# Expert routing on one core: gathers through DRAM exchanged for one-hot matmuls on tokens kept in SBUF

## The reference, cut to what is computed

```python
logits = (t @ w_router + b_router).astype(F32)
top_v, top_i = lax.top_k(logits, TOP_K)                      # 4 of 32
wts = jax.nn.softmax(top_v, axis=-1)
combine = jnp.sum(jax.nn.one_hot(top_i, N_EXPERTS) * wts[..., None], axis=1)
...
y = clamped_swiglu(t @ wu + bu) @ wd + bd                    # per expert: 1024 -> 2048 -> 1024
return acc + cw[:, None].astype(t.dtype) * y
...
x = x + gt2 * moe_ffn(h, ...)                                # then a final RMSNorm
```

## Time and profile before

| | us |
|---|---|
| median of three runs | 1377.89 |
| the profiled execution, its own time | 1376.65 |
| its span, first to last instruction | 1375.0 |
| first expert matmul starts | 366.82 |
| last down matmuls start, 16 records | 1330.96 |
| TensorE busy in the span | 1108.3 (81%) |
| VectorE, ScalarE, GpSimd busy | 274.8, 187.0, 124.5 |
| mean granted TensorE clock | 0.915 of full speed |
| bytes moved by DMA | 481.22 MB, mean 350 GB/s |

### The profile page before, as it was taken

One profiled execution on the slowest core, in us unless ns is written; L12 is line 12 of the kernel. 1 busy time (PEld: TensorE's weight loads), 2 busy tenths in 40 slices (PEclk: granted clock), 3 DMA queues, 4 the chain that ended last, 5 costly groups with the idle time before them and its releaser, 6 DMA issues.

```text
span 1375.0 us, 14665 instructions
## 1 busy us (share of the span) xinstructions
PE 1108.3 (81%) x5751; PEld 471.5 (34%) x5751; DVE 274.8 (20%) x597; ACT 187.0 (14%) x312; POOL 124.5 (9%) x195
## 2 busy tenths in 40 slices
PE   3699688884399888988888888888888888888872
PEld 0388565463133322322222322222222222322221
DVE  1310456465311100101110110101110110101116
ACT  2100632111001101010110101010110101010101
POOL 5000120013200001010000001010000101010003
PEclk8599879886699999999999999999999999999996
DMA  9844259226499999999999999999999999999964
GB/s 350 278 129 145 73 187 351 106 85 211 159 428 414 426 428 427 428 426 426 428 428 427 427 428 425 430 426 426 429 428 427 427 428 426 428 427 427 428 245 157
DMA packets 60656, 481.22 MB, mean 350 GB/s; under 512 B 9469, under 2 KB 21325, under 8 KB 32694
## 3 DMA queue, kind: packets, MB, share of 16 engines
q1 hardware_dynamic: 43936, 444.64, 78.0%
q0 software_dynamic: 10496, 24.18, 5.0%
q10 hardware_dynamic: 6198, 12.03, 2.4%
HBM read 467.38 MB, written 14.28 MB: 350 GB/s over the span
## 4 chain that ended last, share of the span: by engine, by line
DMA 60%; PE 28%; DVE 5%; issue 2%; ACT 2%; POOL 1%; ACTq 0%; SPq 0%; POOLq 0%; PEldq 0%; DVEq 0%
DMA arena<-in_w_up 29%; DMA arena<-in_w_down 28%; PE bank L1127 8%; PE bank L818 6%; PE bank L1147 5%; DMA ring<-in_w_ada 2%; PE bank L969 2%; PE bank L769 2%; PE bank L907 1%; PE bank L786 1%; PE bank L826 1%; PE bank L870 1%; POOL ring L539 1%; PE bank L1000 1%; DMA arena<-mods 0%
## 5 line engine op out<-in xcount | busy, mean ns | idle before, releaser
L1127 PE MATMUL bank<-ring,arena 128*64 128x512 f32 x1536 | 379.5, 641 | 91.0 <-ACT arena L745 51.2
L1127 PEld LDWEIGHTS bank<-ring,arena 128*64 128x64 f32 x1536 | 113.4, 147 | 329.8 <-issue 260.9
L1622 DVE TENSOR_SCALAR arena<-bank 128x256 f32<-128x256 f32 x64 | 24.2, 420 | 614.1 <-PE bank L1127 614.1
L769 PE MATMUL bank<-const,arena 128*128 128x128 f32 (+3 forms) x415 | 74.4, 319 | 77.1 <-DMA arena<-h_rows,idx 21.3
L1147 PE MATMUL bank<-arena 128*64 128x512 f32 x512 | 115.9, 595 | 20.9 <-DMA arena<-in_w_down 20.9
L1127 PE MATMUL bank<-arena 128*64 128x512 f32 x512 | 116.3, 597 | 16.5 <-DMA arena<-in_w_up 15.7
L1147 PE MATMUL bank<-ring,arena 128*64 128x512 f32 x512 | 116.1, 595 | 0.0
L769 PEld LDWEIGHTS bank<-const,arena 128*128 128x128 f32 (+3 forms) x415 | 58.5, 201 | 124.0 <-issue 69.9
L748 ACT ACTIVATE arena<-arena 128x512 f32<-128x512 f32 x32 | 20.2, 631 | 469.8 <-DVE arena L1622 469.8
L514 POOL DMA_DIRECT2D arena<-in_b_up x32 | 16.1, 503 | 745.9 <-PE bank L1147 745.9
L818 PE MATMUL bank<-ring,arena 128*128 128x256 f32 x352 | 81.1, 390 | 0.6 <-issue 0.6
(11 more groups left out here) (293 smaller groups left out, 726.6 us busy)
## 6 DMA issues: line engine op xcount, KB each, us to landing
ring<-in_w_up SPq DMA_DIRECT2D x96, 2048.0 KB, 25.2
arena<-in_w_up SPq DMA_DIRECT2D x32, 2048.0 KB, 28.1
ring<-in_w_down SPq DMA_DIRECT2D x32, 2048.0 KB, 24.3
arena<-in_w_down SPq DMA_DIRECT2D x32, 2048.0 KB, 25.4
ring<-in_w_ada SPq DMA_DIRECT2D x24, 1024.0 KB, 7.4
ring<-in_w_in SPq DMA_DIRECT2D x11, 1024.0 KB, 10.8
y_rows<-arena ACTq DMA_DIRECT2D x64, 128.0 KB, 8.3
ring<-in_w_out SPq DMA_DIRECT2D x4, 1024.0 KB, 5.7
```

The costliest lines, as they stand in the source:

```text
L769: return pe.transpose(out, in_, ident[0:rows, 0:rows])
L1127: mm = pe.matmul(B[2 * e + c % 2][64 * a:64 * a + 64, :], lhsT=xT[:, k, 64 * e:64 * e + 64], rhs=big(n)[:, CH * r + 512 * c:CH * r + 512 * ...
L1622: ins = dve.tensor_scalar(glu[:, 256 * b:256 * (b + 1)], u[:, :, 0], LIMIT, None, ALU.min)
```

## The change

Nothing of routing, token rows or expert outputs goes through DRAM any more.

- **Slots.** `rk1` holds rank + 1 of each token in each chosen expert, 0 elsewhere. For a pair, `build_rows` compares it with the constants 1..64 and gives G, a one-hot matrix tokens x 128 slots. After each pair the two columns are lowered by 64, for the next pass.
- **Picking.** h2 stays in SBUF. Instead of the gather and 8 transposes, `pick_up_rows` makes xT directly: for each of 8 k, three accumulating matmuls (prompt tiles of 128 tokens and the sample tile of 8) of h against G, into banks 0 and 1. It is done for the next pair in the middle of this pair's first down projection.
- **Returning.** GW = G times the routing weights is turned by three transposes (`turn_weights`) into Wc, slots x 264 tokens, copied by ACT. y is copied out to `ysb` by ACT and DVE, half each. `combine_step` multiplies Wc by ysb for the pair before, in four full matmuls of 512 columns and two with 32-column stationary tiles, spread over k = 2..6 of the first expert's up projection. DVE adds each of the five parts to `moe` or `moe_s`.
- **Biases.** b_up of a pair comes in one DMA; the bias of the down projection goes in once as a 33rd "expert": ysb starts as b_down, Wc as the routing weights by expert.
- **The end.** The last pair's sum, the residual and the gate are added on TensorE: six identity matmuls, then four and two of the last Wc. The first norm sums are taken in halves, and the stores are halved and shared by SP and ACT.
- **Layout.** Tiles of the loop lie elsewhere in the arena, which grows from 29300 to 29400 columns; POOL clears moe, moe_s and ysb, in place of the bias clears by DVE.

```diff
@@ picking (TensorE) @@
-                pe.wait_ge(sem("x_full"), it * 16 + 16)
-                pe.wait_ge(sem("gT_copied"), it * 2 + 1)
-                for k in range(KT):
-                    mm = turn(B[6 + k // 4][:, P * (k % 4):P * (k % 4 + 1)],
-                              xg.rearrange("p (c n r) -> p c r n", c=UPS, r=UP_ROWS)[:, c, r, :], P)
+            def pick_up_rows(pair_built):
+                pe.wait_ge(sem("g_built"), pair_built)
+                for k in range(KT):
+                    c, r = divmod(k, UP_ROWS)
+                    for t in range(3):
+                        mm = pe.matmul(B[k // 4][:, P * (k % 4):P * (k % 4 + 1)],
+                                       lhsT=h[0:NT[t], t, :].rearrange("p (c n r) -> p c r n", c=UPS, r=UP_ROWS)[:, c, r, :],
+                                       rhs=G[0:NT[t], t, :, :].rearrange("p e s -> p (e s)"), start=(t == 0), stop=(t == 2),
+                                       skip_group_check=True)
@@ returning (TensorE) @@
+                def combine_step(n):
+                    if n == 0:
+                        pe.wait_ge(sem("wc_copied"), it + 1)
+                        pe.wait_ge(sem("y_copied_a"), it * 2 + 1)
+                        pe.wait_ge(sem("y_copied_d"), it * 2 + 1)
+                    if n >= 2:
+                        pe.wait_ge(sem("sum_added"), it * 5 + n)
+                    if n < 4:
+                        t, a = divmod(n, 2)
+                        mm = combine(B[4 + n % 2][:, :], slice(P * t, P * (t + 1)), a)
+                    else:
+                        for a in range(2):
+                            mm = combine(B[4][32 * a:32 * a + 32, :], slice(S, S + 32), a)
+                    mm.then_inc(sem("sum_made"), 1)
...
+                        if e == 0 and 2 <= k < 7:
+                            combine_step(k - 2)
+                        if e and k == 2:
+                            turn_weights()
                         if e and k == 4:
                             turn_g(0)
...
-                    pe.wait_ge(sem(f"y_copied{e}"), it + 1)
-                    for a in range(2):
-                        pe.matmul(B[4 + e][64 * a:64 * a + 64, :], lhsT=one,
-                                  rhs=bias[e][:, FF2 + 512 * a:FF2 + 512 * (a + 1)],
+                    if e == 0:
+                        pe.wait_ge(sem("wc_copied"), it + 2)
...
                         if e == 0 and k == 4:
+                            pe.wait_ge(sem("u_read"), it * 2 + 2)
+                            pick_up_rows(it + 2)
                             turn_g(1)
@@ the loop's new work on DVE @@
+                dve.wait_ge(sem("xT_made"), it * 2 + 2)
+                dve.tensor_tensor(GW, G, wide(wd[:, :, pair].unsqueeze(3), 3, SLOTS), ALU.mult).then_inc(sem("gw_built"), 1)
+                dve.tensor_scalar(rk1[:, :, pair], rk1[:, :, pair], -float(SLOTS), None, ALU.add).then_inc(sem("rank_lowered"), 1)
+                build_rows(after).then_inc(sem("g_built"), 1)
+                for n in range(5):
+                    dve.wait_ge(sem("sum_made"), it * 5 + n + 1)
...
+                    dve.tensor_tensor(acc, acc, part, ALU.add).then_inc(sem("sum_added"), 1)
@@ POOL @@
-                    pool.dma_start(idx[:, :], list_dram[bass.ds(it * P, P), :]).then_inc(sem("idx_full"), 16)
-                    pool.indirect_dma_start(
-                        out=xg, out_offset=None, in_=h2_dram,
-            for t in range(3):
-                for k in range(TOPK):
-                    pool.indirect_dma_start(
-                        out=yk[t][k][0:NT[t], :], out_offset=None, in_=y_dram,
+                pool.wait_ge(chunks_used, it * PER + (PRE + 2 * UPS))
+                up_bias((it + 1) % PAIRS)
+            for t in range(2):
+                pool.tensor_tensor(moe[:, t, :], moe[:, t, :], gate2, ALU.mult).then_inc(sem("x2_part"), 1)
@@ ACT @@
-                for a in range(2):
-                    act.dma_start(y_dram[bass.ds(i * P + 64 * e, SLOTS), 512 * a:512 * (a + 1)],
+                    act.activation(ysb[r, e, :], B[4 + e][r, :], ACT.Copy).then_inc(sem("y_copied_a"), 1)
```

More of the change, by code:

```diff
@@ L236, in hybrid_layer @@
         wr = take(KT * E, z_at + 5 * D).rearrange("p (k e) -> p k e", k=KT)
[L238 to L259, removed]
+        bias = take(FF2, z_at)
+        ysb = take(2 * 512, z_at + 2 * D).rearrange("p (a n) -> p a n", a=2)
+        ysg = take(2 * 512, z_at + 3 * D).rearrange("p (a n) -> p a n", a=2)
@@ new lines, in hybrid_layer @@
+        xT = take(D, zs_at + 512).rearrange("p (k t) -> p k t", k=KT)
+        glu, lin, sg = (take(512, zs_at + 512 + D + 512 * n) for n in range(3))
+        gg = [take(512, hT_at + 512 * n) for n in range(2)]
+        gT = [take(512, hT_at + 1024 + 512 * n) for n in range(2)]
+        moe = take(2 * D, hT_at + 2304).rearrange("p (t c) -> p t c", t=2)
+        more_ring = take(4 * CH, ada_at)
+        gate2 = take(D, ada_at + 4 * CH)
+        rows2s = take(2 * D, ada_at + 4 * CH + D)
+        g_fin = take(D, ada_at + 4 * CH + 3 * D)
@@ L493, in _ @@
+            up_bias(0)
             pool.wait_ge(sem("npass_ready"), 1)
             passes = pool.value_load(npass[0:1, 0:1], min_val=1, max_val=MAXPASS)
[L495 to L502, removed]
-                    pool.dma_start(idx[:, :], list_dram[bass.ds(it * P, P), :]).then_inc(sem("idx_full"), 16)
-                    pool.wait_ge(sem("idx_full"), it * 16 + 16)
-                    pool.nop(nofuse=True)
-                    pool.indirect_dma_start(
-                        out=xg, out_offset=None, in_=h2_dram,
[L508 to L532, removed]
@@ new lines, in _ @@
+            with pool.Fori(0, total) as it:
+                pool.wait_ge(chunks_used, it * PER + (PRE + 2 * UPS))
+                up_bias((it + 1) % PAIRS)
+            pool.wait_ge(sem("sum_added"), total * 5 + 1)
+            for t in range(2):
+                pool.tensor_tensor(moe[:, t, :], moe[:, t, :], gate2, ALU.mult).then_inc(sem("x2_part"), 1)
+            for t in range(2):
+                pool.wait_ge(sem("x2_part"), t + 1)
+                pool.tensor_tensor(moe[:, t, :], moe[:, t, :], x[:, t, :], ALU.add).then_inc(sem("x2_part"), 1)
@@ L544, in _ @@
+            pool.wait_ge(sem("bias_full"), total * 16 + 16)
         @block.scalar
@@ L755, in _, with copy_rows @@
-            for n, t in enumerate(LAST):
-                act.wait_ge(sem("x2_ready"), n + 1)
-                act.activation(moe[0:NT[t], t, :], x[0:NT[t], t, :], ACT.Square,
-                               accum_out=ssum3[0:NT[t], t:t + 1]).then_inc(sem("sums"), 1)
-                act.wait_ge(sem("means"), 6 + n + 1)
-                root(t)
+            total = act.snap(passes * PAIRS)
+            def copy_rows(made):
+                act.wait_ge(sem("xT_made"), made)
+                act.activation(xT[:, 4:8, :], B[1][:, :].rearrange("p (k t) -> p k t", k=4), ACT.Copy).then_inc(sem("xT_copied_a"), 1)
@@ new lines, in _ @@
+            act.activation(sg[0:1, 0:1], root3[0:1, 0:1], ACT.Sqrt)
+            for t in range(2):
+                for a in range(2):
+                    act.wait_ge(sem("x2_made"), 2 * t + a + 1)
+                    act.activation(moe[:, t, 512 * a:512 * (a + 1)], B[2 * t + a][:, :], ACT.Square, accum_out=half_sum[:, t, a:a + 1]).then_inc(sem("half_sums"), 1)
+                act.wait_ge(sem("half_means"), t + 1)
+                act.wait_ge(sem("half_sums"), 2 * t + 2)
+                act.activation(root3[:, t:t + 1], half_sum[:, t, 1:2], ACT.Sqrt, scale=1.0 / D, bias=half_mean[:, t:t + 1]).then_inc(sem("roots"), 1)
@@ L763, in _ @@
+            act.wait_ge(sem("x2_ready"), 1)
+            act.activation(h[0:NB, 1, :], h[0:NB, 2, :], ACT.Square, accum_out=ssum3[0:NB, 2:3]).then_inc(sem("sums"), 1)
+            act.wait_ge(sem("means"), 7)
+            root(2)
+            for n in range(2):
+                act.wait_ge(sem("result"), n + 3)
+                act.dma_start(O["yp"][0, P:S, 512 * n:512 * (n + 1)], x[:, 1, 512 * n:512 * (n + 1)]).then_inc(sem("result_stored"), 16)
         @block.tensor
@@ L1556, in number @@
[L1556 to L1560 removed]
+                dve.wait_ge(sem("chosen_ready"), nth)
@@ new lines, in number, with weigh_tokens @@
+                link(dve.scalar_tensor_tensor(out=rk1[r, ts, :], in0=ranks.rearrange("p (t e) -> p t e", t=nt), scalar=1.0,
+                                              in1=chosen[r, ts, :], op0=ALU.add, op1=ALU.mult))
+            def weigh_tokens(ts, r, exps):
+                nt = len(range(3)[ts])
+                dve.wait_ge(sem("top_exp"), exps)
+                link(dve.tensor_tensor(wd[r, ts, :], ex[r, ts, :], chosen[r, ts, :], ALU.mult))
+                link(dve.tensor_reduce(tsum[r, ts], wd[r, ts, :], AX.X, ALU.add))
+                link(dve.reciprocal(tsum[r, ts], tsum[r, ts]))
+                link(dve.tensor_tensor(wd[r, ts, :], wd[r, ts, :], wide(tsum[r, ts].unsqueeze(2), 2, E), ALU.mult))
@@ L1596, in _ @@
```

(26 more changed lines are left out.)

341 lines of the change are left out of this document (146 added, 195 removed).

## The result

| | before | after |
|---|---|---|
| median, us | 1377.22 (4 runs) | 1386.26 (4 runs, 1384.93 to 1386.51) |
| span of the profiled execution | 1375.0 | 1384.5 |
| first expert matmul starts | 366.82 | 365.06 |
| from there to the last down matmul's end | 967.8 | 999.1 |
| from there to the end of the span | 40.4 | 20.4 |

The ratio is 1.0064, with a 95% interval of 1.0047 to 1.0082: slower by 0.6%, where 4.5% faster was forecast. The table already says where: the end gives back 20 us, where 18 were forecast, the start gives 1.8 instead of 9, and the loop, which was to give 34, takes 31.

What follows compares the result with a forecast made beforehand. The old loop was taken as DMA-bound, with TensorE some 15% below; after the change TensorE would narrowly decide. Start 357.5, loop 934, end 22 and 1.65 outside the span gave 1315 us, range 1292 to 1350.

Steps and rivals of the forecast that it cites:

- DMA per pair, 58.9 us: Loop: weights take the share freed by gathers, indexes and y stores, so a pair's transfers fall from 61.80 to 58.9 us.
- TensorE decides: Loop: with six chunks ready at the start, TensorE should hardly starve and sets the time, 16 x 58.4 = 934 us.
- TensorE per pair, 58.4 us: Loop: 46.2 us of remaining old work plus picking, combines, transposes and switches sum to 58.4 us a pair.
- Picking: Loop: 24 picking matmuls a pair at 0.272 us each, priced from L907, 6.5 us.
- Full combines and switches: Loop, per pair: four full matmuls 3.6 us, two with 32-column tiles 0.9, seven more switches between matmul kinds 0.7.
- The bounds: Loop: picking takes no less than 3.7 us a pair, and 12.4 if loads and matmuls run one after the other.
- rival 4: Loop: picks' loads don't hide, 12.4 instead of 6.5 us; 64.3 us a pair, 1410 us in all; chance 0.08.
- The start, 357.5: Before the loop: first up matmul at 357.5 us against 366.8, with the first picking slowed to 8.0 us.
- No waits, no clock loss in steady pairs: Loop: the 3.38 us wait for xT and its slow start go; new waits are covered, clock 1.00 in steady windows.
- rival 3: Loop: a new wait replaces the removed one; 1 to 3.4 us a pair gives 1331 to 1369 us; chance 0.15.
- The end, 22 us: After the last down matmul: 22 us to the end of the span, against 40.4; bounds 18 and 27.
- seven times: At the end: POOL's four operations of 1024 columns, 1.3 us each on DVE, may be seven times dearer.

Runs made afterwards that it cites:

- e3_no_returning: Changed kernel without the five combine steps and DVE's adds for all pairs but the last (result incomplete): 1320.09 us, one run.
- e6_all: Changed kernel with 128-row sample tile, three combine groups, 128-row up bias, POOL's last bias load left out: 1307.95 us, ratio 0.9504 to the kernel before.
- e2_pad: Changed kernel with the sample tile picked over 128 rows, the unfilled ones cleared, order unchanged: 1331.12 us, ratio 0.9676 to the kernel before.
- e5_group: Changed kernel with its five combine steps in three groups (two, two, one), same matmuls: 1375.44 us, one run.
- e1_order: Changed kernel with the same picks sorted by height, 16 of 128 rows, then 8 of 8 rows: 1359.27 us, ratio 0.9875 to the kernel before.

## Why the prediction was wrong, step by step

The profiled run took 71 us more than the 1315 forecast: 65 in the loop, 7.6 at the start, and 1.6 less at the end. Of the 65, 62 are 16 pairs at 62.27 instead of 58.4, and 3 are the slow first up matmuls.

- **DMA per pair, 58.9 us**: right. e3_no_returning and e6_all show 58.85 and 58.87.
- **"TensorE decides"**: right, and more than meant: no wait in the chain, DMA at 403 GB/s.
- **TensorE per pair, 58.4 us**: wrong, 62.27. This is the step that failed, by terms that were mis-sized. *Picking*, 6.5: measured 8.75. L907 is a run of equal 128-row matmuls, and for such a run its price was even 0.65 too high (5.85 in e2_pad). But every third pick has 8 rows, and the changes of height, which the sum put at nothing, cost 2.90. In all that is +2.25. *Full combines and switches*, 3.6 + 0.9 + 0.7 = 5.2: measured 4 x 1.06 + 0.98 + 5 x 0.15 (the up matmuls behind each visit) + 0.15 (those behind the three transposes) = 6.1, +0.9. " show none to speak of" looked at switches between tiles of one width; for a change of width the sum had only the transposes' 0.1 on entry, and I should have kept a higher bound. *The up bias*, not in the sum: I took off the down bias and did not see that the up bias went from 128 rows to one. The earlier trace rows have its old price, 1.72; the new is 1.86 and 1.87 behind it: +0.6. Together 3.75 of the 3.87 missing.
- **The bounds**: the 8.75 of picking lay between the bounds 3.7 and 12.4, and rival 4 named the point from which it decides, 62.2 us a pair; the pair took 62.27 and the kernel is 0.6% slower. That the point was met so closely is chance: it was the mark for loads that do not hide, and the missing time came from other terms. In e2_pad 48 loads of full tiles and their 48 matmul records fit in 5.85 us together. The Trainium skill, TensorE: Matmul & The Clock Gate, Part 3, "What overlaps and what doesn't", has loads overlap matmuls only in other row groups. By that the padded picks, all over the same 128 rows, could not overlap and would be dear; they are the cheap ones, so the trace disagrees. The outcome between my forecast and that rival had no case of its own, so the range ended at 1350.
- **The start, 357.5**: wrong, 365.06. TensorE began picking at 349.16, 0.5 late; then 15.04 us instead of 8.0, and 6.24 for 16 records that take 3.43. I took the slow start of the earlier trace rows, which was of one width and height, as a fixed price. e2_pad, where picking takes 7.83 us and the first up matmul comes at 356.84, shows that the estimate holds for matmuls of one height.
- **No waits, no clock loss in steady pairs**: right; the clock is 1.00 from 700 to 1180. All new handoffs between engines were covered, so rival 3 did not come.
- **The end, 22 us**: 20.4. POOL's operations took 2.3 each, not 1.3, within my "seven times". What they did to DVE I had not asked.

## What to carry to other kernels

When a transfer-bound loop is to be relieved by work on another engine, that engine's slack is the whole budget (here about 9 of 62 us a pair), so price the new work in the sequence in which it runs, not from a run of equal instructions. On TensorE put matmuls of one height and one width next to each other, and pad a small tile with zeros where that keeps the height; here 120 rows of zeros were worth 4%. When work moves to GpSimd, ask which VectorE operations run beside it.

## What the runs showed of the hardware that I had not expected

- Between neighbouring float32 picks over 128 columns, each change of height from 128 to 8 rows or back costs about 0.19 us (8.75 against 6.04 us, 14 changes fewer); with 32 rows picking costs the same as with 8 (8.75). For the bias matmuls over 512 columns with one row it is 0.15 a change.
- Going from 64-column tiles to a full 128-column matmul and back costs 0.35 us (0.20 in, 0.15 out, e5_group).
- TensorE can be busy without a pause and be held at or fall to half speed: 0.50 for the 15.04 us of mixed picks, 0.57 behind 16 records in a row over 8 rows in e1_order. With 128 rows throughout it rose during the first picking (7.83 us), and mixed picks that began at 1.00 kept it. Which property of the work counts is open.
- A VectorE operation with two inputs in SBUF took 9.69 instead of 0.69 us while four GpSimd operations of 2.3 us ran.
